# Diffusion backbone: Q, K and V ahead of the Fourier projection, attention units between its slabs, three conditioning units as TensorE products

## The chip, the cores and the metric

The kernel runs on one core of one Trainium2 chip. The metric is the device time of one execution in microseconds (us); lower is better. Five engines run side by side, each through its own instructions in order, and wait for each other by semaphores: TensorE (PE, matrix products into PSUM), VectorE (DVE), ScalarE (ACT), GpSimd (POOL), and SyncE (SP), which here only issues DMAs. All of the weights come from HBM once per execution.

## The reference, cut to what matters

Two layers over 256 tokens of width 2048, float32, and 256 context tokens. The change is in layer 0, the attention layer:

```
mod   = silu(c) @ w_mod[0] + b_mod[0]        # six vectors of 2048: shift, scale, gate (mixer), shift, scale, gate (MLP)
ux    = rmsnorm(x)*g0 * (1 + sc_m) + sh_m    # the same for the context, with silu(c_ctx)
f, q, k, v = split(ux @ att_w_in, [1024, 2048, 2304])      # 1024 Fourier columns, 1024 Q, 256 K, 256 V
k_c, v_c   = split(uc @ att_w_in[:, 2048:])
q, k  = rope(q), rope(k)
attn  = sink_softmax(window(q k^T), q k_c^T) @ [v, v_c]    # 8 heads, 2 KV heads, head 128
four  = real(fft over tokens and over the 256 channels of each of 4 groups of f)
x     = x + gt_m * rmsnorm(concat(four, attn) @ att_w_out)
x     = x + gt_f * rmsnorm(relu(modulate(x) @ w1)^2 @ w2)
```

Layer 1 has a short gated convolution instead of attention, and the same kind of MLP.

## The kernel before

**Weights.** Each product is computed to nearly float32 precision from a high and a low part. A weight *slab* is 256 rows by 512 columns, 512 KB: SP loads it into `raw` (4 slots), ScalarE writes its high part to `whi` (`hi`, line 716), VectorE the rest to `wlo` (`lo`, line 1014), TensorE takes three products: high by high, high by low, low by high. 8 slabs make a *group*, 512 output columns (`slab_of`, line 42, gives a group's first slab). `group_slab` (line 463) leaves channels on the partitions; `token_group` (line 520) leaves tokens there, with 12 products of 512 columns per slab. Slab w may be loaded when slab w - 4 is lowered, and split when slab w - 4 is used.

**Conditioning.** The vectors are products of one row with `w_mod`. A *unit* is half a vector: 16 slabs of 128 x 1024, 512 KB each. The first four units (mixer shift and scale) are TensorE products in the start phase (line 485), for both conditioning vectors, out of a ring in `early` (the memory of `h`): two products per slab with 32 stationary columns, each at its own column tile. The other 20 (`UNITS`) are VectorE's: `unit_slab` (line 1019) adds slab times scalar to `acc`; then GpSimd sums over partitions (line 1596) and, for a vector wanted by channel, multiplies by the identity; `finish_unit` (line 1072) reduces that and adds the bias. A gate is wanted by row and needs only the sum, `finish_gate` (line 1083). The slabs go through `mraw` (2 slots), or in attention through the 4 slots of `raw` (line 348).

**Layer 0's order.** Groups: two Fourier, two of Q, one of K and V with the context (`group_kv`, line 557), then attention with the DFTs, then four output groups. `UNIT_SHARE = (4, 6, 7, 7, 14)` puts 38 unit slabs beside the five input groups on VectorE (`att_group`, line 1220), the last 14 of them behind the last weight slab of the K and V group. VectorE copies K and rotates it behind these. `fin` holds the Fourier projection by channels. In attention, a *unit* `un` is one head and one half of the queries, 16 in all. TensorE's loop (line 648) has for each: transposes of the probabilities, `scores` of unit un + 3, one DFT part, and each second time the products with V. VectorE's loop (line 1285) has for each: denominator, maximum of unit un + 2, then three unit slabs of the 42 left. The transform over channels comes first, then that over tokens. V comes by channels, is copied and transposed (line 645). The output groups start when all of attention and the Fourier part is there (line 657).

The queues' order is what the program writes: SP issues loads in the order in which VectorE frees the slots, and waits in place; the units of the MLP and convolution stages run beside their weight slabs, with the same functions and places before and after the change.

Of the kernel before, what the change touches and what calls it, by code (L numbers as in the profile page):

```python
# [7 lines left out]
ALU = mybir.AluOpType  # L8
# [4 lines left out]
P = 128  # L13
# [22 lines left out]
PG_F, PG_Q, PG_KV, PG_WO = 0, 2, 4, 5  # L36
PG_MLP = (9, 57)
PG_CONV, PG_CO = 41, 53
W_F, W_KV = 0, 32


def slab_of(pg):

    return SL * pg + W_F
# [4 lines left out]
         (1, 3, 0), (1, 3, 1), (1, 4, 0), (1, 4, 1), (1, 5, 0), (1, 5, 1)]  # L49
GATES = (3, 4, 6, 11, 12, 13, 18, 19)  # L50
# [12 lines left out]
def by_tokens(pg):  # L63

    return PG_WO <= pg < PG_WO + 4 or PG_CO <= pg < PG_CO + 4 or any(
        pg0 <= pg < pg0 + 32 and (pg - pg0) % 8 >= 4 for pg0 in PG_MLP)
# [12 lines left out]
def masks_before(un):  # L79

    return un - sum(1 for g in GATES if g < un)

# [6 lines left out]
def backbone_program(nc, x_in, c_in, ctx_in, c_ctx, w_mod, b_mod, gains, att_w_in, sink, att_w_out,  # L89
                     conv_w_in, conv_w, conv_w_out, mlp_w1, mlp_w2, tables, out):  # L90
    with ExitStack() as ctx:
# [52 lines left out]
        fin = y[:, 8:16, :]  # L144
        qh = fq[:, 0:8, :]
        vsum = yf[:, 1024:2048].rearrange("p (g t) -> p g t", g=2)
        prob = [yf[:, 512 * i:512 * i + 512] for i in range(2)]
        probT = [ff[:, 2048 + 1024 * i:3072 + 1024 * i].rearrange("p (k q) -> p k q", k=4) for i in range(2)]
        ucs = yf[:, 1024:2048].rearrange("p (k n) -> p k n", k=2)
        row = (red[:, :], acc[:, 1, :])  # L150

        yt = yf.rearrange("p (a d) -> p a d", a=2)
        whole = [tmp[a][:, :, :].rearrange("p c t -> p (c t)") for a in range(2)]
# [19 lines left out]
        mid_landed = [sem(f"mid_landed{i}") for i in range(SLOTS)]  # L173
# [18 lines left out]
        v_t, v_ready = sem("v_t"), sem("v_ready")  # L192
# [52 lines left out]
        def _(sp):  # L245
# [21 lines left out]

            def w_slab(wt, row0, col0, s):
                return wt[bass.ds(row0 + s * CPS * P, CPS * P), bass.ds(col0, GW)].rearrange("(c p) n -> p c n", p=P)
# [20 lines left out]
            def stage_loads(w0, wt, row0, col0, un, n_m, l, mcol, ahead, early=False, gate_un=None):  # L290
# [3 lines left out]
                for i in range(4):  # L294
                    source = ahead if i == 3 else group_slabs(wt, row0, col0 + (i + 1) * GW)
                    k0, at = UNIT_EARLY[i] if early else (4 * i, UNIT_AT)
                    load_step(w0 + SL * (i + 1), source, un * UNIT + k0, k0, l, mcol, at if n_m else ())
# [4 lines left out]
            for w in range(START_SLABS):  # L302
                hv, k = divmod(w, KC)
                col0 = (1 - hv // 2) * D + (hv % 2) * HALF
                if w == START_F:
                    for s in range(SLOTS):
                        load_slab(W_F + s, s, group_slabs(att_w_in[0], 0, 0)(s))
# [10 lines left out]
            wi, wo = att_w_in[0], att_w_out[0]  # L318
# [17 lines left out]
            for s in range(SLOTS, SL):  # L336
                load_slab(W_F + s, s % SLOTS, group_slabs(wi, 0, 0)(s))

            m = 0
            for i in range(5):  # L340
                for s in range(SL):
                    if i < 4:
                        load_slab(W_F + SL * (i + 1) + s, s % SLOTS, group_slabs(wi, 0, (i + 1) * GW)(s))
                    for j in unit_places(i, s):
                        load_unit_slab(m + j, (m + j) % 2, 0, (m + j) % UNIT, mcol((m + j) // UNIT))
                m += UNIT_SHARE[i]

            for m in range(M_MID, M_WO):
                slot = (m - M_MID) % SLOTS
                if m < M_MID + SLOTS:  # L350
                    sp.wait_ge(lo_ready, W_KV + SLOTS + slot + 1)
                else:
                    sp.wait_ge(m_used, m - (SLOTS - 1))
                sp.dma_start(raw[:, slot, :], w_mod[0, m % UNIT * P:(m % UNIT + 1) * P,
                                                    mcol(m // UNIT):mcol(m // UNIT) + HALF]
                             ).then_inc(mid_landed[slot], 16)
            for s in range(SLOTS):
                sp.wait_ge(m_used, M_WO - (M_WO - 1 - M_MID - s) % SLOTS)
                load_slab(slab_of(PG_WO) + s, s, w_slab(wo, 0, 0, s))
            for s in range(SLOTS, SL):  # L360
                load_slab(slab_of(PG_WO) + s, s % SLOTS, w_slab(wo, 0, 0, s))
# [3 lines left out]
            stage_loads(slab_of(PG_WO), wo, 0, 0, U_WO, 4, 0, mcol(U_WO), group_slabs(mlp_w1[0], 0, 0), True,  # L365
# [25 lines left out]
            for t, (un, n_m, k0) in enumerate(CONV_PARTS):  # L391
                for j in range(3):
                    wt, col0 = ((ci, 2 * D + t * GW), (ci, t * GW), (ci, D + (t + 1) * GW) if t < 3 else (co, 0))[j]
                    w = slab_of(PG_CONV + 3 * t + j + 1)
                    for s in range(SL):
                        load_slab(w + s, s % SLOTS, w_slab(wt, 0, col0, s))
                        for i in conv_unit_slabs(SL * j + s, n_m):
                            load_unit_slab(UNIT * un + k0 + i, i % 2, 1, k0 + i, mcol(un))
# [13 lines left out]
        def _(pe):  # L412
# [65 lines left out]
            def first_group_slab(s):  # L478

                pe.wait_ge(lo_ready, W_F + s + 1)  # L480
                pe.wait_ge(u_ready, s + 1)
                group_slab(PG_F, 0, u, s)
# [37 lines left out]
            def token_group(pg, slot, src, slab_waits, closing=False):  # L520
# [4 lines left out]
                def products(s, a):  # L525
                    for c in range(CPS):
                        k = s * CPS + c
                        high = src[:, k, a * P:(a + 1) * P]
                        low = src[:, k, T + a * P:T + (a + 1) * P]
                        cols = slice(c * GW, (c + 1) * GW)  # L530
                        o = ps[:, 4 * slot + a, :]
                        pe.matmul(o, high, whi[:, s % SLOTS, cols], start=(k == 0), stop=False)  # L532
                        pe.matmul(o, high, wlo[:, s % SLOTS, cols], start=False, stop=False)  # L533
                        last = pe.matmul(o, low, whi[:, s % SLOTS, cols], start=False, stop=(k == KC - 1))  # L534
# [22 lines left out]
            def group_kv():  # L557


                for s in range(SL):  # L560
                    pe.wait_ge(lo_ready, W_KV + s + 1)
                    pe.wait_ge(c_ready, s // 2 + 1)
                    for c in range(CPS):
                        k = s * CPS + c
                        for m in range(4):
                            cols = slice(c * GW + m * P, c * GW + (m + 1) * P)
                            for i, src in enumerate((u, h)):
                                o = ps[:, 2 * i + m // 2, m % 2 * T:(m % 2 + 1) * T]
                                pe.matmul(o, whi[:, s % SLOTS, cols], src[:, k, 0:T], start=(k == 0 and m % 2 == 0),
# [1114 lines left out]
```

## Time and profile before

| | us |
|---|---|
| median of 3 runs (lowest, highest) | 2394.24 (2388.2, 2400.92) |
| the profiled execution | 2392.11 |
| its span (first to last instruction) | 2390.3 |
| TensorE busy | 2212.3 |
| weight loads (PEld) busy | 1832.3 |
| VectorE busy | 1736.6 |
| ScalarE busy | 994.9 |
| GpSimd busy | 180.9 |

Mean memory traffic is 248 GB/s, mean granted TensorE clock 0.964 of 2.4 GHz. Busy times of engines overlap, and TensorE's contain pipelined products whose ends are modelled. In a timeline row the number in brackets is idle time of the engine ahead of the piece, and what ended it; L427 and the like are lines of the kernel. Products of plain float32 operands appear as two instructions (x2) for each product. Stages of the span, from the timelines: start phase to 126.8 us; Fourier and Q groups to 209; K and V to 260.5; attention and DFTs 282.4 to 402.9; output groups 403.9 to about 506; the MLP of layer 0 from 526 us.

### The profile page before, as it was taken

The numbers are of one execution on the slowest core, as the hardware profiler recorded it, in microseconds if no ns is written. First come the engines' busy times: TensorE is split into PE (matmuls) and PEld (weight loads), VectorE is DVE, ScalarE is ACT, GpSimd is POOL, SyncE is SP. The second block draws the span as 40 slices with busy tenths as digits, with TensorE's granted clock in tenths as the row PEclk, the third lists the DMA queues.
The fourth block names the chain that finished last, engine by engine and source line by source line (L and its number), as shares of the span: only waits on it lengthen the run. The fifth ranks groups of instructions, "written<-read, shape, count | busy, mean of one in ns | idle before, by whom it ended". The sixth has DMA issues, their size and how long they took to land.

```text
span 2390.3 us, 30891 instructions
## 1 busy us (share of the span) xinstructions
PE 2212.3 (93%) x11279; PEld 1832.3 (77%) x11279; DVE 1736.6 (73%) x1830; ACT 994.9 (42%) x1214; POOL 180.9 (8%) x56
## 2 busy tenths in 40 slices
PE   6899577969999999999989999996999999999998
PEld 3488445758888888888878888875888888888886
DVE  0278595878879877978888998787887655555565
ACT  2155144434434434434444444433443443443443
POOL 0001020110102101101110110011010100000000
PEclk8999788989999999999999999998999999999999
DMA  9977576748888888888876787774888666656654
GB/s 377 347 251 251 177 234 205 266 150 278 287 288 276 278 293 275 276 296 300 277 274 222 274 298 272 244 262 153 284 278 303 186 191 191 187 190 193 204 192 142
DMA packets 253899, 592.67 MB, mean 248 GB/s; under 512 B 18082, under 2 KB 18610, under 8 KB 253234
## 3 DMA queue, kind: packets, MB, share of 16 engines
q1 hardware_dynamic: 253746, 590.63, 73.7%
q8 instruction: 96, 1.57, 0.3%
q14 instruction: 57, 0.47, 0.1%
HBM read 588.46 MB, written 2.10 MB: 247 GB/s over the span
## 4 chain that ended last, share of the span: by engine, by line
PE 75%; DVE 11%; DMA 6%; issue 5%; ACT 2%; POOL 1%; SPq 0%; DVEq 0%; ACTq 0%; POOLq 0%
PE ps L471 27%; PE ps L472 14%; PE ps L532 10%; PE ps L533 10%; PE ps L534 10%; DVE acc L1033 5%; DVE wlo L1017 2%; PE ps L427 2%; DMA early<-in_w_mod_dram 2%; DMA mraw<-in_w_mod_dram 2%; PE ps L498 1%; ACT whi L721 1%; POOL red L1596 1%; DMA raw<-in_conv_w_out_dram 1%; DMA raw<-in_att_w_out_dram 1%
## 5 line engine op out<-in xcount | busy, mean ns | idle before, releaser
L1017 DVE TENSOR_TENSOR wlo<-raw,whi 128x1024 fp32r<-128x1024 f32 x712 | 927.8, 1309 | 469.3 <-ACT whi L721 468.3
L721 ACT ACTIVATE whi<-raw 128x1024 fp32r<-128x1024 f32 x712 | 750.1, 1058 | 973.3 <-PE ps L534 380.1
L471 PE MATMUL ps<-u,whi 128*128 128x512 f32 x3072 | 1085.9, 398 | 13.6 <-DVE wlo L1017 11.3
L472 PE MATMUL ps<-u,wlo 128*128 128x256 f32 x3072 | 862.4, 281 | 0.0
L471 PEld LDWEIGHTS ps<-u,whi 128*128 128x128 f32 x3072 | 577.7, 188 | 159.0 <-DVE wlo L1017 12.5
L472 PEld LDWEIGHTS ps<-u,wlo 128*128 128x128 f32 x3072 | 581.4, 189 | 0.2
L532 PE MATMUL ps<-whi,h 128*128 128x512 f32 x1152 | 452.5, 393 | 16.4 <-DVE wlo L1017 16.4
L533 PE MATMUL ps<-wlo,h 128*128 128x512 f32 x1152 | 451.3, 392 | 0.0
L534 PE MATMUL ps<-whi,h 128*128 128x512 f32 x1152 | 450.9, 391 | 0.0
L1033 DVE SCALAR_TENSOR_TENSOR acc<-mraw,cs,acc 128x1024 f32<-128x1024 f32 x278 | 363.7, 1308 | 22.7 <-DMA mraw<-in_w_mod_dram 22.4
L532 PEld LDWEIGHTS ps<-whi,h 128*128 128x128 f32 x1152 | 218.1, 189 | 64.6 <-DVE wlo L1017 19.0
L534 PEld LDWEIGHTS ps<-whi,h 128*128 128x128 f32 x1152 | 218.1, 189 | 45.9
L533 PEld LDWEIGHTS ps<-wlo,h 128*128 128x128 f32 x1152 | 218.2, 189 | 45.0
L1596 POOL PARTITION_ALL_REDUCE red<-acc x20 | 129.1, 6457 | 1467.0 <-DVE acc L1033 612.7
L819 ACT ACTIVATE tmp<-ps 128x512 f32<-128x512 f32 x96 | 56.6, 596 | 42.3 <-PE ps L472 42.3
L427 PE MATMUL ps<-diag,x 128*128 128x128 f32 x256 | 39.9, 312 | 35.1 <-DVE diag L1126 35.1
L427 PEld LDWEIGHTS ps<-diag,x 128*128 128x128 f32 x256 | 36.5, 223 | 43.7 <-DVE diag L1126 36.3
L1033 DVE SCALAR_TENSOR_TENSOR acc<-raw,cs,acc 128x1024 f32<-128x1024 f32 x42 | 65.1, 1550 | 3.7
L532 PE MATMUL ps<-whi,u 128*128 128x512 f32 x128 | 52.4, 409 | 9.9 <-DVE wlo L1017 8.9
L498 PE MATMUL ps<-early,junk 128*32 128x512 f32 x192 | 42.2, 682 | 18.5 <-DMA early<-in_w_mod_dram 18.5
L957 ACT ACTIVATE h<-fq 128x512 fp32r<-128x512 f32 x64 | 39.5, 633 | 29.8 <-DVE fq L1445 29.8
L533 PE MATMUL ps<-wlo,u 128*128 128x512 f32 x128 | 51.6, 403 | 0.0
(149 smaller groups left out, 1195.5 us busy)
## 6 DMA issues: line engine op xcount, KB each, us to landing
raw<-in_mlp_w_dram SPq DMA_DIRECT2D x512, 512.0 KB, 4.6
mraw<-in_w_mod_dram SPq DMA_DIRECT2D x278, 512.0 KB, 5.0
raw<-in_conv_w_in_dram SPq DMA_DIRECT2D x96, 512.0 KB, 5.1
raw<-in_w_mod_dram SPq DMA_DIRECT2D x58, 512.0 KB, 4.7
early<-in_w_mod_dram SPq DMA_DIRECT2D x48, 512.0 KB, 9.8
raw<-in_att_w_in_dram SPq DMA_DIRECT2D x40, 512.0 KB, 5.4
raw<-in_att_w_out_dram SPq DMA_DIRECT2D x32, 512.0 KB, 5.9
raw<-in_conv_w_out_dram SPq DMA_DIRECT2D x32, 512.0 KB, 6.2
```

The source lines that it names most:

```text
L427: last = pe.matmul(ps[:, bank, c * T + a * P:c * T + (a + 1) * P], src[:, a, k * P:(k + 1) * P], diag[:, d0 + a, :], start=True, stop=True)
L471: pe.matmul(bank, whi[:, s % SLOTS, cols], src[:, k, :], start=(k == 0), stop=False)
L472: last = pe.matmul(bank[:, 0:T], wlo[:, s % SLOTS, cols], src[:, k, 0:T], start=False, stop=(k == KC - 1))
L498: last = pe.matmul(ps[tile:tile + 32, (0, 2, 0, 6)[hv] + n, :], crs[:, k, :], start_slab(w)[:, n * 512:(n + 1) * 512], start=(k < 4), stop ...
L532: pe.matmul(o, high, whi[:, s % SLOTS, cols], start=(k == 0), stop=False)
L533: pe.matmul(o, high, wlo[:, s % SLOTS, cols], start=False, stop=False)
L534: last = pe.matmul(o, low, whi[:, s % SLOTS, cols], start=False, stop=(k == KC - 1))
L721: act.activation(whi[:, s, :], raw[:, s, :], ACT.Copy).then_inc(hi_ready, 1)
L819: act.activation(tmp[half][:, :, :], right(slot, half), ACT.Copy).then_inc(b_copied, 1)
L1017: dve.tensor_tensor(wlo[:, s, :], raw[:, s, :], whi[:, s, :], ALU.subtract).then_inc(lo_ready, 1)
L1033: dve.scalar_tensor_tensor(out=a, in0=src, scalar=cs[:, bass.ds(k, 1)], in1=a, op0=ALU.mult, op1=ALU.add).then_inc(m_used, 1)
L1596: pool.partition_all_reduce(red[:, :], acc[:, un % 2, :], P, RADD).then_inc(unit_summed, 1)
```

## The change

Layer 0's order is changed; what lies behind its output groups is as before, but for slab counters.

- *Groups*: Q, Q, K and V, then Fourier, Fourier (`ATT_COLS` gives each group's first column). The Fourier groups are taken by tokens, so that the transform over tokens can come first (`token_dft`), then that over channels (`channel_dft`); V is taken by tokens too, and its transposes and copies through `vsum` go.
- *One loop of 24 steps*, t = 0..23, on TensorE, VectorE and ScalarE (25 there): a Fourier slab in steps 0 to 15 and one of the eight DFT parts of `DFT_ORDER` in steps 16 to 23; transposes of attention unit t - 4, scores of unit t - 2, in each second step the products with V; then conditioning slabs. In Fourier slabs banks 4 and 5 are used, scores alternate between banks 0 and 1, bank 2 has the transposes, 3 the attention output, 6 and 7 the conditioning products. The attention output goes to `h`, channels 8 to 15.
- *Conditioning*: units 3, 4 and 2 (`MIX_UNITS`) are TensorE products (`mix_slab`), two slabs per step, loaded into four slots of `early`, which is `h`'s memory and so only free when the K and V group is done. Units 0 and 1 are VectorE's, one slab per step up to step 15, two from 16 to 23; the first slab of each writes `acc`, the rest add to it. GpSimd takes no part in units 0 to 4. `unit_columns` turns units 0, 1 and 2 into columns by 24 products of two columns in slab 1 of the first output group; `spread_gate` spreads units 3 and 4 over the partitions by a product with a one-row matrix.
- *Output groups*: their slabs come attention half first (`OUT_ORDER`), waiting for each Fourier group in the second half. The loop has the lower halves of the first four of them.

The diff, cut to its core:

```diff
-PG_F, PG_Q, PG_KV, PG_WO = 0, 2, 4, 5
+PG_Q, PG_KV, PG_F, PG_WO = 0, 2, 3, 5
+ATT_COLS = (1024, 1536, 2048, 0, 512)
+MIX_UNITS = (3, 4, 2)
+DVE_FIRST = 2
+POOL_FIRST = 5
...
@@ SP
+            def mix_pair(n):
+                for i in (2 * n, 2 * n + 1):
+                    if i >= SLOTS:
+                        sp.wait_ge(mix_used, i - (SLOTS - 1))
+                    un, k = MIX_UNITS[i // UNIT], i % UNIT
+                    sp.dma_start(early[:, i % SLOTS, :], w_mod[0, k * P:(k + 1) * P, mcol(un):mcol(un) + HALF]
+                                 ).then_inc(mix_landed[i % SLOTS], 16)
...
+            for w in range(SLOTS, W_F + 6):
+                att_slab(w)
+            first_unit_slab(0)
+            first_unit_slab(1)
+            for t in range(-1, 17):
+                att_slab(W_F + t + 7)
+                if t == -1:
+                    sp.wait_ge(slab_used, W_KV + SL)
+                mix_pair(t + 1)
+                if t >= 0:
+                    first_unit_slab(t + 2)
+            for t in range(17, 23):
+                mix_pair(t + 1)
+                first_unit_slab(2 * t - 15)
+                first_unit_slab(2 * t - 14)
+            first_unit_slab(31)
             sp.wait_ge(o_ready, HEADS)
             sp.wait_ge(f_ready, FG)
             gate_rows(3)
...
@@ TensorE
+            def mix_slab(n):
+                i, k = divmod(n, UNIT)
+                if k == 0 and i:
+                    pe.wait_ge(mix_copied, i)
+                pe.wait_ge(mix_landed[n % SLOTS], 16 * (n // SLOTS + 1))
+                for half in range(2):
+                    tile = 32 * ((k + 2 * half) % 4)
+                    last = pe.matmul(ps[tile:tile + 32, 6 + half, :], crs[:, k, :],
+                                     early[:, n % SLOTS, half * 512:(half + 1) * 512], start=(k < 4),
+                                     stop=(k >= KC - 4), tile_position=(0, tile))
+                last.then_inc(mix_used, 1)
...
+            for t in range(24):
+                if t < 2 * SL:
+                    fourier_slab(t)
+                else:
+                    stage_dft, g = DFT_ORDER[t - 2 * SL]
+                    (channel_dft if stage_dft else token_dft)(g)
+                if 0 <= t - 4 < 2 * HEADS:
+                    turn_probs(t - 4)
+                if 0 <= t - 2 < 2 * HEADS:
+                    scores(t - 2)
+                if t >= 7 and t % 2 and t // 2 - 3 < HEADS:
+                    values(t // 2 - 3)
+                for n in mix_slabs(t):
+                    mix_slab(n)
...
+            def unit_columns():
+                pe.wait_ge(mix_copied, 3)
+                pe.wait_ge(m_used, DVE_FIRST * UNIT)
+                for un, src, pick in ((0, acc[:, 0, :], ones[:, 0:2]), (1, acc[:, 1, :], ones[:, 0:2]),
+                                      (2, mix_row[2], sel)):
+                    for c in range(KC // 2):
+                        last = pe.matmul(ps[:, 6, 16 * un + 2 * c:16 * un + 2 * c + 2], src[:, c * P:(c + 1) * P],
+                                         pick, start=True, stop=True)
+                last.then_inc(columns_done, 1)
+            def out_waits(s):
+                if s == 0:
+                    pe.wait_ge(o_ready, HEADS)
+                if s == 1:
+                    unit_columns()
+                    pe.wait_ge(pt_copied, 2 * HEADS)
+                    spread_gate(0, 2)
+                if s >= SL // 2:
+                    pe.wait_ge(f_ready, s - SL // 2 + 1)
+                if s == SL // 2 + 1:
+                    pe.wait_ge(mod_ready, 3)
+                    spread_gate(1, 6)
...
@@ ScalarE
+            for t in range(25):
+                if t in MIX_COPIES:
+                    copy_mix_row(MIX_COPIES.index(t))
+                if t <= 16:
+                    hi(W_F + 3 + t, (3 + t) % SLOTS)
+                if 0 <= t - 3 < 2 * HEADS:
+                    probabilities(t - 3)
+                if 0 <= t - 5 < 2 * HEADS:
+                    probs_turned(t - 5)
+                if t >= 8 and t % 2 == 0 and t // 2 - 4 < HEADS:
+                    o_high(t // 2 - 4)
+                if 0 <= t - 3 < 2 * HEADS:
+                    normalized(t - 3)
+                if 0 <= t - 2 * SL < 2 * FG:
+                    stage_dft, g = DFT_ORDER[t - 2 * SL]
+                    (fourier_high if stage_dft else token_transformed)(g)
...
@@ VectorE
+            for t in range(25):
+                if t in (SL, 2 * SL):
+                    take_fourier(t // SL - 1)
+                if 0 <= t - 3 < 2 * HEADS:
+                    row_max(t - 3)
+                if t <= 16:
+                    lo(W_F + 3 + t, (3 + t) % SLOTS)
+                if 0 <= t - 3 < 2 * HEADS:
+                    denominator(t - 3)
+                for m in first_unit_slabs(t):
+                    first_unit_slab(m)
+                if t >= 8 and t % 2 == 0 and t // 2 - 4 < HEADS:
+                    o_low(t // 2 - 4)
+                if 0 <= t - 2 * SL < 2 * FG and DFT_ORDER[t - 2 * SL][0]:
+                    fourier_low(DFT_ORDER[t - 2 * SL][1])
+            finish_first()
...
-UNIT_SHARE = (4, 6, 7, 7, 14)
-M_MID, M_WO = sum(UNIT_SHARE), UNIT * U_WO
+OUT_ORDER = tuple((s + SL // 2) % SL for s in range(SL))
+DFT_ORDER = ((0, 0), (0, 1), (1, 0), (0, 2), (1, 1), (0, 3), (1, 2), (1, 3))
+MIX_COPIES = (9, 17, 24)
+def mix_slabs(t):
+    return range(2 * (t - 1), 2 * t) if 1 <= t < 23 else range(44, 48) if t == 23 else ()
+def first_unit_slabs(t):
+    return (t,) if t < 16 else range(2 * t - 16, 2 * t - 14) if t < 24 else ()
```

The context pieces (`context_high`, `context_low`) come two per Q group now. Scores of unit un wait for the probabilities of unit un - 2, transposes for the copy of the ones before, `values` for the `o_low` of the head before.

## Rows read from the trace of the kernel before

**Rows 1.** The page: busy time (share) x instructions; the chain that ended last, by engine.

```profile
PE 2212.3 (93%) x11279; PEld 1832.3 (77%) x11279; DVE 1736.6 (73%) x1830; ACT 994.9 (42%) x1214; POOL 180.9 (8%) x56
...
PE 75%; DVE 11%; DMA 6%; issue 5%; ACT 2%; POOL 1%; SPq 0%; DVEq 0%; ACTq 0%; POOLq 0%
```

**Rows 2.** Busy time by stage: stretch, us, busy time (x instructions), clock, DMA share, GB/s.

```profile
47.00:92.00 45.00, 36.33 (x234) 16.11 (x232) 9.12 (x13) 7.57 (x8) 0.00 (x0) 0.98 0.98 372
...
164.80:187.00 22.20, 22.20 (x130) 19.58 (x129) 19.14 (x18) 13.25 (x17) 0.00 (x0) 1.00 0.90 330
...
212.60:260.50 47.90, 47.80 (x384) 47.62 (x384) 31.47 (x31) 10.35 (x13) 3.29 (x2) 0.96 0.66 207
260.50:282.40 21.90, 0.02 (x1) 0.02 (x1) 11.53 (x11) 5.27 (x9) 0.00 (x0) 0.60 0.72 240
282.40:404.00 121.60, 82.65 (x265) 50.99 (x266) 99.59 (x144) 49.99 (x116) 25.83 (x8) 0.83 0.62 199
```

**Rows 3.** The chain of waits in order of time: start us, us, what.

```profile
242.49 5.99 DMA mraw<-in_w_mod_dram
```

**Rows 4.** TensorE's timeline: start, us, line, shape, count, idle before and its releaser.

```profile
203.53 0.50 PE L471 MATMUL ps<-u,whi 128*128 128x512 f32 x1 [2.16 <-DVE wlo L1017]
...
212.68 0.36 PE L569 MATMUL ps<-u,whi 128*128 128x256 f32 x1 [3.23 <-DVE wlo L1017]
282.38 5.49 PE L598 MATMUL ps<-kv,fq 128*128 128x512 f32 x6 [21.91 <-DVE kv L1218]
```

**Rows 5.** Who waited for whom, 282 to 404 us: us in total, times, longest.

```profile
PE ps L606 <- ACT y L860: 36.9, 13, 6.5
ACT y L860 <- DVE sm L1271: 23.0, 11, 5.6
...
SPq L354 <- DVE acc L1033: 88.1, 38, 16.1
```

**Rows 6.** VectorE's timeline.

```profile
276.95 0.68 DVE L1250 COPY y<-ps 128x512 f32<-128x512 f32 x1
...
281.64 0.69 DVE L1218 TENSOR_TENSOR kv<-y 128x512 f32<-128x512 f32 x1
...
408.05 1.23 DVE L1017 TENSOR_TENSOR wlo<-raw,whi 128x1024 fp32r<-128x1024 f32 x1 [4.26 <-ACT whi L721]
410.77 1.23 DVE L1017 TENSOR_TENSOR wlo<-raw,whi 128x1024 fp32r<-128x1024 f32 x1 [1.50 <-ACT whi L721]
...
420.08 1.28 DVE L1033 SCALAR_TENSOR_TENSOR acc<-mraw,cs,acc 128x1024 f32<-128x1024 f32 x1
...
511.95 1.22 DVE L1077 TENSOR_REDUCE t<-red 128x8 f32<-128x1024 f32 x1 [10.05 <-POOL red L1601]
```

**Rows 7.** TensorE's operations one by one, from the same view of other stretches.

```profile
49.68 1.95 PE L438 MATMUL ps<-tab,red 128*128 128x2 f32 x16 [1.11 <-ACT red L761]
...
105.02 1.07 PE L498 MATMUL ps<-early,junk 128*32 128x512 f32 x8
106.01 0.50 PE L471 MATMUL ps<-u,whi 128*128 128x512 f32 x1
...
310.42 0.60 PE L606 MATMUL ps<-tab,y 128*128 128x128 f32 x4
...
310.85 1.02 PE L598 MATMUL ps<-kv,fq 128*128 128x512 f32 x2
...
311.71 1.89 PE L635 MATMUL ps<-tab,y 128*128 128x256 f32 x8
...
313.44 1.89 PE L615 MATMUL ps<-fq,kv 128*128 128x256 f32 x8
...
317.59 1.88 PE L624 MATMUL ps<-tab,y 128*128 128x512 f32 x4
```

**Rows 8.** The page's DMA issues: count, KB each, median us to landing.

```profile
mraw<-in_w_mod_dram SPq DMA_DIRECT2D x278, 512.0 KB, 5.0
...
early<-in_w_mod_dram SPq DMA_DIRECT2D x48, 512.0 KB, 9.8
```

More of the change, by code:

```diff
@@ L79, in masks_before, with first_slab @@
 def masks_before(un):
-    return un - sum(1 for g in GATES if g < un)
+    return un - POOL_FIRST - sum(1 for g in GATES if POOL_FIRST <= g < un)
+def first_slab(un):
+    return (un - len(MIX_UNITS)) * UNIT
 def unit_col(u):
@@ L348, in _ @@
[L348 to L356, printed above, removed]
@@ L640, in _ @@
-            for un in range(3):
-                scores(un)
-            pe.wait_ge(kv_copied, 3)
-            for kv in range(KV_HEADS):
-                for kt in range(4):
-                    last = pe.transpose(ps[:, kv, kt * P:(kt + 1) * P], vsum[:, kv, kt * P:(kt + 1) * P], ident)
-                last.then_inc(v_t, 1)
-            pe.wait_ge(v_ready, KV_HEADS)
-            for un in range(2 * HEADS):
-                turn_probs(un)
-                if un + 3 < 2 * HEADS:
-                    scores(un + 3)
-                (channel_dft if un % 4 < 2 else token_dft)(un // 4, un % 2)
-                if un % 2 == 1 and un >= 3:
-                    values(un // 2 - 1)
@@ L655, in _, with token_dft @@
-            values(HEADS - 1)
-            pe.wait_ge(f_ready, FG)
-            pe.wait_ge(o_ready, HEADS)
+            def token_dft(g):
+                pe.wait_ge(sum_done, sums_before(PG_F) + 2 * (g // 2 + 1))
+                if g == 0:
+                    pe.wait_ge(sum_done, sums_before(PG_F) + 4)
+                else:
+                    pe.wait_ge(fa_copied, 4 * g)
+                for m in range(2):
+                    for a in range(2):
+                        last = pe.matmul(ps[:, 4 + m, :], fin[:, a, g * T + m * P:g * T + (m + 1) * P], dft[:, a, :],
+                                         start=(a == 0), stop=(a == 1))
+                    last.then_inc(fa_done, 1)
@@ new lines, in spread_gate @@
+            def spread_gate(i, bank):
+                pe.wait_ge(first_row_ready, 1)
+                for n in range(2):
+                    last = pe.matmul(ps[:, bank + n, :], first_row, mix_row[i][:, n * 512:(n + 1) * 512],
+                                     start=True, stop=True)
+                last.then_inc(gate_spread, 1)
+            def unit_columns():
[7 more added lines that the diff above has]
+                last.then_inc(columns_done, 1)
@@ L1245, in _ @@
             dve.wait_ge(tab_landed, 32)
-            for i in range(5):
-                att_group(i)
+            for i in range(2):
+                query_group(i)
+            for s in range(3):
+                lo(W_F + s, s)
             dve.wait_ge(slab_used, W_KV + SL)
@@ L1618 @@
 CONV_PARTS = ((14, 16, 0), (15, 16, 0), (16, 8, 0), (16, 8, 8))
-def unit_places(i, s):
-    n = UNIT_SHARE[i]
-    return range(s * n // SL, (s + 1) * n // SL)
 def conv_unit_slabs(i, n_m):
```

393 lines of the change are left out of this document (202 added, 191 removed).

## The prediction, made before the changed kernel was built or run

> **What bounds the kernel now.** I read the page first: TensorE is busy for 93% of the span and owns 75% of the chain that ended last [rows 1]. Such a kernel gains only where TensorE is not working, so I asked next for busy time by stage [rows 2]. In the projection groups up to 209 us TensorE is busy but for short waits. The key and value group (212.6 to 260.5 us) is full too, by weight loads: 47.62 of 47.9 us. Then come the two loose stretches. From 260.5 to 282.4 us TensorE does nothing (0.02 us); from 282.4 to 404.0 us, in attention with the DFTs, it is busy 82.65 of 121.6 us, at a granted clock of 0.83. Together these are 143.5 us (260.5 to 404.0). The chain of waits says why in the first one: VectorE waits for one conditioning slab after the other, such as the one of 5.99 us [rows 3]. TensorE itself starts again 21.91 us late, for the rotated keys that VectorE makes only behind these slabs [rows 4]. In the second one TensorE waits for normalized probabilities (36.9 us over 13 waits), ScalarE for VectorE's reciprocals, and the DMA queue for VectorE to free slabs, 88.1 us over 38 waits [rows 5]. VectorE, with 99.59 of 121.6 us busy, sets the order. The memory is not full there: DMA share 0.62, 199 GB/s [rows 2].
>
> **The change part by part.** The working is against the profiled execution: span 2390.3 us, its own time 2392.1 us; the median of the runs, 2394.2 us, is 0.1% above that.
>
> *Front: Q, K, V ahead of the Fourier groups.* Two Fourier groups of 22.2 us (two windows alike, 142.6:164.8 and 164.8:187.0, one shown [rows 2]) leave the stretch before K and V: -44.4 us, to be paid back below. No conditioning slab lies in this stretch any more, so VectorE, which ran such slabs ahead of the weight halves that TensorE waited for 2.16 and 3.23 us [rows 4], has none of them: -5.4 us. What is late next there is TensorE's own work; the second context piece per group costs ScalarE and VectorE a few us beside groups in which they are busy 13.25 and 19.14 of 22.2 us, slabs included [rows 2]. If that cover failed, the loss would be the same 5 us again. K and V keep their 384 products of 256 columns; V by tokens only swaps the operands: 47.9 us, no change. So K and V end 49.8 us earlier, at about 211 us.
>
> *The joint stretch: 24 steps of TensorE.* It holds, at full clock:
> - 16 Fourier slabs of 12 products of 512 columns. The output projection has the same slab, and its lower halves follow TensorE at 2.72 us, from 408.05 to 410.77 [rows 6]: 43.5 us.
> - 16 transposes of probabilities at 0.43 us, 16 scores at 0.86, 8 value products at 1.73, and 16 DFT parts (8 of each kind, same counts as before) at 1.73 [rows 7], start to start, the value product taken as long as the DFT part since both show 1.89 us busy: 6.9 + 13.8 + 13.8 + 27.7 = 62.2 us.
> - 48 conditioning slabs as products, in 24 pairs. A pair in the start phase takes from 105.02 to 106.01 us, 0.99 us [rows 7], though it is eight products of 512 columns: their 32-column tiles run side by side. 23.8 us. These are new on TensorE.
> The sum is 129.5 us. The eight V transposes go.
>
> The granted clock: it was 0.83 where TensorE was 68% busy, 0.96 to 1.00 where it was full [rows 2]. Here it should be about 85% busy; I take 0.93, so 129.5 / 0.93 = 139 us. The Trainium skill has a rule that speaks against the change here (TensorE: Matmul & The Clock Gate, "HAM oscillation"): short bursts of products with DMA waits between them fall back to 1.2 GHz again and again. By that rule the whole would end near rival 3's 2407 us.
>
> To this I add waits, 11 us: about 3 us at the start, since the second pair of conditioning slabs is queued on SP behind a weight slab that needs ScalarE and VectorE to finish keys and rotation first (in the kernel before this took from 276.95 to 282.33 us, VectorE's copy to its last add [rows 6]); 2 us for the two Fourier evictions that must precede the next group in the same banks; 6 us in steps 17 to 23, where SP asks for VectorE's second slab of a step only after TensorE has finished that step's products, it lands about 5.0 us later [rows 8], and the steps' o_low stands behind it on VectorE, for which `values` waits. That gives 150 us.
>
> *The DMA side of it.* From the end of K and V on SP moves 17 weight slabs, 48 slabs into `early` and 30 into `mraw` beside one weight slab loaded ahead: 96 x 0.524 MB = 50.3 MB. At the 372 GB/s of 47:92 [rows 2] this is 135 us, at the 330 GB/s of the 164.8:187.0 window 152 us. So DMA and TensorE are about equal, and 150 us fits both.
>
> *VectorE* there has 32 slabs at 1.28 us and 17 lower halves at 1.23 [rows 6], 62 us. Before, its 99.59 us held 42 slabs and 4 lower halves, 59 us, so attention's own part is some 41 us. Sum about 103 of 150 us, so it is hidden. If it were late by a step, attention's chain would be next (rival 1).
>
> So the loose 143.5 us and the 44.4 us of Fourier become 150 us.
>
> *Output projection.* Its first half of rows is the attention half, so it needn't wait for the last DFTs; this is why I charge no wait at its start. New on TensorE, in its first group: 24 column products. Eight of the same kind took 16 instructions and 1.95 us from 49.68 us on [rows 7]: 5.9 us. Two spread products of two 512-column halves each, at the 0.86 us of a score: 3.4 us. And TensorE waits for VectorE's slab 31, which is asked for only when slab 29 is used: about 2.5 us (none, if TensorE is slower before). Sum +12 us; bounds are 9 without the wait and 18 with the column products at half the clock. SP's `gate_rows(3)` waits behind these columns, and the weight slabs of group 1 behind it on the queue; TensorE then still has 7 slabs of 2.72 us, 19 us, so it isn't late. In return POOL does units 3 and 4 no longer. That was off the path: only the last unit's reduction ends it, VectorE waiting 10.05 us for it until 511.95 [rows 6]. Unit 5, its slabs and this wait stay as they are, so the boundary behind it stays too, and all that follows.
>
> Sum: -49.8 + (150 - 143.5) + 12 = -31 us, so 2361 us.
>
> **The rivals.**
> 1. *The attention chain keeps its pace.* Score, maximum, exponential, reciprocal, scaling, transpose cross five engines; one transpose bank now serves where two did. Before, a unit took 121.6 / 16 = 7.6 us [rows 2]. 24 steps at this pace are 182 us: 2361 + 32 = 2393 us, no change. For it: VectorE still has rows, lower halves and slabs in line. Against: a step now has one slab of VectorE (1.3 us), not three (3.8 us), and the DMA queue's 88 us of waiting for VectorE [rows 5] falls to a third.
> 2. *Everything packs.* DMA at 372 GB/s is the only bound and the waits fall inside: 136 us, and no wait for slab 31: 2361 - 14 - 3 = 2344 us. For it: ten slab buffers keep the queue full. Against: one queue in order, and each of its waits holds all behind it.
> 3. *Slower: TensorE waits for slabs it now consumes itself and runs at the half clock.* Place: `mix_slab`, two per step, in the queue ahead of every other product. In the start phase, where it also ate slabs, the landing took 9.8 us [rows 8]. If it waits in each step, its busy share falls under that of the attention before. At a clock of 0.70, 129.5 / 0.70 + 11 = 196 us: 2407 us. It decides from a clock of 0.71 on (193 us, +12 us); up to 0.76 it only eats the gain. Against it: a pair is asked for two steps ahead, about 10 us, and in 47:92, with TensorE fed in this way, the clock was 0.98.
>
> **How the numbers follow.** Forecast 0.60 (its own range 2348 to 2380 us), rival 1 0.19, rival 2 0.12, rival 3 0.09. About 0.5%, 12 us, is what a measurement of this kernel can tell from no change: under 2380 us is faster, over 2404 slower. Forecast and rival 2 with a little of rival 1 give faster 0.74; the rest of rival 1, same 0.17; rival 3, slower 0.09. The range goes from rival 2 with the low bound of the output term, 2341 us, to rival 1, 2394 us.
>
> **What would show it.** K and V end near 211 us; no idle of 20 us behind it; the first product of the output projection near 361 us; DMA share near 0.9 and a clock over 0.9 in between; that projection some 12 us longer, with 48 small products in it. Were the stretch over 180 us, TensorE's waits would name the cause: for ScalarE's probabilities (rival 1) or for `early` (rival 3). A first stretch that ends after 216 us, or a changed time behind the first boundary, would make the working wrong in a place where I saw nothing.

## The result and the profile after

The changed kernel takes 2380.7 us (median of 10 runs, 2373.63 to 2383.16), the kernel before 2393.7 us (also of 10) beside it: ratio 0.9946, 95% interval 0.9929 to 0.9962, so 13 us faster. The forecast was 31 us. The direction is right and the outer range, 2341 to 2394 us, holds the time, but 2380.7 us lies just outside the forecast's own range of 2348 to 2380 us, and the gain is less than half of the one forecast.

The page of the changed kernel, span 2379.9 us: busy times, and the chain that ended last [rows 1]:

```profile
PE 2239.5 (94%) x11455; PEld 1833.0 (77%) x11455; DVE 1656.3 (70%) x1780; ACT 993.0 (42%) x1211; POOL 140.8 (6%) x43
...
PE 79%; DVE 7%; DMA 7%; issue 3%; ACT 2%; POOL 1%; SPq 1%; DVEq 0%; ACTq 0%; POOLq 0%
```

TensorE has 27 us more of work (new products) in a shorter span. Busy time by stage of the changed kernel, columns as in [rows 2]:

```profile
128.00:211.50 83.50, 82.04 (x577) 77.04 (x578) 43.79 (x50) 47.00 (x64) 0.00 (x0) 0.98 0.52 158
211.50:307.10 95.60, 90.32 (x430) 54.84 (x428) 64.20 (x114) 51.64 (x96) 0.00 (x0) 0.98 0.92 345
307.10:382.30 75.20, 54.49 (x216) 28.62 (x212) 23.63 (x34) 18.38 (x43) 0.00 (x0) 0.89 0.61 219
382.30:511.80 129.50, 106.37 (x440) 85.80 (x440) 85.78 (x104) 44.62 (x68) 11.18 (x5) 0.88 0.60 207
```

From 211.5 to 307.1 us, steps 0 to 15, TensorE is busy 90.32 of 95.6 us, and DMA share and traffic, 0.62 and 199 GB/s in the old attention [rows 2], are 0.92 and 345 GB/s. But from 307.1 to 382.3 us, steps 16 to 23, TensorE is busy 54.49 of 75.2 us, at a clock of 0.89, and the DMA share is back at 0.61. Marks of both kernels, from TensorE's timelines, beside the forecast:

| us from the span's start | before | forecast | after | after less forecast |
|---|---|---|---|---|
| K and V end | 260.5 | 211 | 211.5 | +0.5 |
| step 16 begins | - | 307 | 307.1 | 0 |
| first product of the output projection | 403.9 | 361 | 382.4 | +21 |
| first product of the MLP's boundary | 521.0 | 490 | 511.8 | +22 |
| end of the span | 2390.3 | 2359 | 2379.9 | +21 |

(The 307 of the forecast follows from its own prices: 84.3 of the 129.5 us lie in steps 0 to 15, at 0.93 and with 5 of the 11 us of waits that is 95.6 us.) One stretch, steps 16 to 23, holds nearly the whole error of 21 us. Its chain of waits in the changed kernel (start us, us, what), from TensorE's conditioning pair of step 18 on:

```profile
333.94 1.94 PE ps L652 x8
335.88 0.28 SPq L365
336.20 0.43 SPq L365
336.68 5.61 DMA mraw<-in_w_mod_dram
342.31 1.28 DVE acc L1152
343.59 0.35 DVE h L1396
344.07 3.39 PE ps L683 x8
347.46 1.07 PE ps L652 x8
348.53 0.28 SPq L365
348.86 0.43 SPq L365
349.33 5.65 DMA mraw<-in_w_mod_dram
355.00 1.30 DVE acc L1152
356.32 4.19 DMA mraw<-in_w_mod_dram
360.53 1.29 DVE acc L1152
361.82 0.35 DVE h L1396
362.30 3.75 PE ps L683 x8
366.05 1.77 PE ps L652 x8
```

It is a ring. L652, the conditioning pair at the end of TensorE's step, frees its slots; SP (L365) then issues the next pair, and only behind it VectorE's slabs; one lands 5.6 us later; VectorE adds it (L1152), then makes `o_low` of that step (L1396), for which the value products (L683) of TensorE's next odd step wait; at their end stand the conditioning pair and SP again. Around 335.88 to 348.53 us it takes 12.65 us, and 19.3 us from 348.53 to 367.82, two steps, where two slabs land one after the other (5.65 and 4.19 us). TensorE's work in a step is about 5.6 us.

Until 333 us the ring takes another way back to TensorE. The row maximum of the next attention unit also stands behind the slabs in VectorE's order; ScalarE's exponential waits for it, the copy of the turned probabilities (L980) stands behind that exponential, and TensorE's next transposes (L674) wait for the copy. The turn before the one above:

```profile
323.36 5.37 DMA mraw<-in_w_mod_dram
...
328.75 1.28 DVE acc L1152
...
330.04 0.22 DVE ps L1380
...
330.28 0.70 DVE sm L1382
...
331.01 0.23 DVE sm L1384
...
331.46 0.76 ACT y L967 x2
332.22 0.50 ACT fq L980
...
332.85 1.09 PE ps L674 x4
```

The waits of 307 to 383 us name both places (us, times, longest): 9.3 us for `o_low` and 8.3 us for the copy. The DMA rates in 40 slices of 305 to 382 us show bursts at 400 GB/s between zeros:

```profile
DVE acc L1152 <- DMA mraw<-in_w_mod_dram: 49.0, 8, 10.2
...
PE ps L683 <- DVE h L1396: 9.3, 2, 5.6
PE ps L674 <- ACT fq L980: 8.3, 2, 6.7
```

```profile
GB/s 400 175 326 402 349 334 404 36 0 66 355 417 251 0 4 9 64 387 419 219 0 0 0 219 404 423 383 385 264 100 0 0 0 202 415 413 347 358 328 126
```

### The profile page after: what moved, and what is told of

It is laid out like the page before. It is cut to its first block, busy times and chain, and to the rows that moved or that the text cites. A ratio compares the mean times of both kernels' runs of the same rounds, so it can differ in the third digit from the quotient of the medians.

```text
span 2379.9 us, 31101 instructions
## 1 busy us (share of the span) xinstructions
PE 2239.5 (94%) x11455; PEld 1833.0 (77%) x11455; DVE 1656.3 (70%) x1780; ACT 993.0 (42%) x1211; POOL 140.8 (6%) x43
## 4 chain that ended last, share of the span: by engine, by line
PE 79%; DVE 7%; DMA 7%; issue 3%; ACT 2%; POOL 1%; SPq 1%; DVEq 0%; ACTq 0%; POOLq 0%
PE ps L497 26%; PE ps L498 13%; PE ps L560 10%; PE ps L562 10%; PE ps L561 10%; DMA mraw<-in_w_mod_dram 3%; DVE wlo L1129 2%; PE ps L453 2%; DVE acc L1139 2%; DMA early<-in_w_mod_dram 2%; PE ps L524 1%; ACT whi L827 1%; DMA raw<-in_conv_w_in_dram 1%; DMA raw<-in_mlp_w_dram 1%; PE ps L683 1%
## 5 line engine op out<-in xcount | busy, mean ns | idle before, releaser
L497 PE MATMUL ps<-u,whi 128*128 128x512 f32 x2944 | 1040.2, 398 | 12.9 <-DVE wlo L1129 10.2
L498 PE MATMUL ps<-u,wlo 128*128 128x256 f32 x2944 | 825.3, 280 | 0.0
L497 PEld LDWEIGHTS ps<-u,whi 128*128 128x128 f32 x2944 | 554.3, 188 | 152.7 <-issue 12.1
L498 PEld LDWEIGHTS ps<-u,wlo 128*128 128x128 f32 x2944 | 557.3, 189 | 0.2
L560 PE MATMUL ps<-whi,h 128*128 128x512 f32 x1216 | 477.2, 392 | 18.2 <-DVE wlo L1129 16.2
L561 PE MATMUL ps<-wlo,h 128*128 128x512 f32 x1216 | 475.3, 391 | 0.0
L562 PE MATMUL ps<-whi,h 128*128 128x512 f32 x1216 | 475.3, 391 | 0.0
L560 PEld LDWEIGHTS ps<-whi,h 128*128 128x128 f32 x1216 | 229.7, 189 | 70.0 <-DVE wlo L1129 18.8
L562 PEld LDWEIGHTS ps<-whi,h 128*128 128x128 f32 x1216 | 229.5, 189 | 48.2
L1732 POOL PARTITION_ALL_REDUCE red<-acc x15 | 96.7, 6446 | 1248.2 <-DVE acc L1139 558.4
L1152 DVE SCALAR_TENSOR_TENSOR acc<-mraw,cs,acc 128x1024 f32<-128x1024 f32 x30 | 38.5, 1284 | 65.3 <-DMA mraw<-in_w_mod_dram 65.0
L1574 DVE TENSOR_TENSOR fq<-ps,tmp 128x512 f32<-128x512 f32 x64 | 43.1, 686 | 10.4 <-ACT tmp L925 10.4
L1031 ACT ACTIVATE fq<-tmp 128x512 f32<-128x512 f32 x32 | 20.0, 624 | 61.3 <-DVE tmp L1452 38.3
```

The source lines that it names most:

```text
L497: pe.matmul(bank, whi[:, s % SLOTS, cols], src[:, k, :], start=(k == 0), stop=False)
L498: last = pe.matmul(bank[:, 0:T], wlo[:, s % SLOTS, cols], src[:, k, 0:T], start=False, stop=(k == KC - 1))
L560: pe.matmul(o, high, whi[:, s % SLOTS, cols], start=first, stop=False)
L1732: pool.partition_all_reduce(red[:, :], acc[:, un % 2, :], P, RADD).then_inc(unit_summed, 1)
```

## The experiments

Theory: SP's one queue, in order, ties VectorE's slabs to TensorE's step end, and VectorE's order ties `o_low` and the row maxima to the slabs. Rivals: the memory can't deliver the bytes of these steps, or the DFT parts, handed between TensorE and ScalarE, set 9 us a step. Medians below stand beside 2393.6 to 2395.1 us of the kernel before in the same sessions.

**SP's order in steps 17 to 22.**

```diff
             for t in range(17, 23):
-                mix_pair(t + 1)
                 first_unit_slab(2 * t - 15)
                 first_unit_slab(2 * t - 14)
+                mix_pair(t + 1)
```

> SP's order alone, steps 17 to 22: the two VectorE slabs are asked for before the TensorE pair. Queue theory (the pair's wait for the end of TensorE's step holds the VectorE slabs behind it, these hold o_low, and o_low holds the value products): steps 16 to 23, 75 us in the changed kernel, fall to 52 to 60 us, and the kernel to 2358 to 2366 us. Bandwidth theory (the slabs' bytes fill the memory): order changes nothing, 2381 us. DFT theory (TensorE and ScalarE hand the transforms to and fro at some 9 us a step): nothing, 2381 us.

2360.72 us, ratio 0.9867 (0.9849 to 0.9884). The output projection begins at 365.1 instead of 382.4 us, and steps 16 to 23 last 57.3 instead of 75.3 us. The same bytes in the same queue, another order: 17 us on the trace, 20 in the median. Its row from 307.1 to 360 us, columns as in [rows 2]:

```profile
307.10:360.00 52.90, 47.41 (x204) 26.44 (x196) 23.81 (x35) 16.44 (x41) 0.00 (x0) 0.97 0.88 306
```

The memory moves 306 GB/s there, so it could deliver all along; and the DFT parts were not touched. Both rivals fall as the cause of these 17 us. The ring isn't wholly gone: TensorE still waits 1.59 and 2.15 us for `o_low`.

**VectorE's order from step 16 on**: `o_low` and `fourier_low` ahead of the step's slabs.

```diff
-                for m in first_unit_slabs(t):
-                    first_unit_slab(m)
+                if t < 2 * SL:
+                    for m in first_unit_slabs(t):
+                        first_unit_slab(m)
...
                     fourier_low(DFT_ORDER[t - 2 * SL][1])
+                if t >= 2 * SL:
+                    for m in first_unit_slabs(t):
+                        first_unit_slab(m)
```

> VectorE's order alone, from step 16 on: o_low and fourier_low before the step's slabs. Queue theory: the waits of TensorE's value products for o_low (3.7 and 5.6 us) and for the output projection go, but VectorE still falls behind on its slabs, so the last row maxima stay late: 8 to 12 us less, 2369 to 2373 us. Bandwidth and DFT theory: 2381 us.

2371.74 us, 0.9910 (0.9893 to 0.9926): 9 us off, as the queue theory had it. The waits for `o_low` are gone; the one in front of the last transposes, the ring's other way, stays:

```profile
331.91 1.08 PE L674 MATMUL ps<-tab,y 128*128 128x128 f32 x4 [6.79 <-ACT fq L980]
```

Steps 16 to 23 last 61.6 us here, 13.7 less than in the changed kernel, but some of it is lost again behind them: the column products wait 3.75 us for slab 31, where it was 1.70 us.

**Both orders.**

> Both orders together. Queue theory: the last steps run at TensorE's own work of some 49 us plus DMA, little better than the SP order alone: 2355 to 2364 us. Bandwidth and DFT theory: 2381 us.

2361.07 us, 0.9858 (0.9842 to 0.9875), equal to SP's order alone, and steps 16 to 23 last 57.2 us. SP's order acts on both ways of the ring, VectorE's only on the one through `o_low`. With both the last waits for `o_low` are gone too, but the last pair for TensorE now comes later in SP's queue, and its wait takes their place:

```profile
360.93 3.21 PE L652 MATMUL ps<-early,junk 128*32 128x512 f32 x8 [3.87 <-DMA early<-in_w_mod_dram]
```

**Without the loads.** SP's loads of slabs 17 to 31 go, and VectorE doesn't wait:

```diff
-                dve.wait_ge(m_landed[m % 2], 16 * (m // 2 + 1))
+                if m < 17:
+                    dve.wait_ge(m_landed[m % 2], 16 * (m // 2 + 1))
+                else:
+                    src = acc[:, 0, :]
```

> The loads of VectorE's slabs 17 to 31 are left out, and VectorE takes its own accumulator in their place (conditioning units 1 and the mixer's output thus wrong). Queue theory: no slab to wait for, the last eight steps take some 50 us: about 2355 us. Bandwidth theory: the same, 15 of 31 slabs gone, so this run and the order runs together separate the two. DFT theory: the steps stay near 9 us, 2375 us or more.

2355.11 us, 0.9832 (0.9809 to 0.9854). Its row of the same stretch:

```profile
307.10:360.00 52.90, 51.92 (x238) 29.67 (x238) 27.29 (x37) 19.62 (x44) 0.00 (x0) 1.00 0.53 174
```

From step 16 to the output projection it takes 48.8 us (306.9 to 355.8). TensorE's own work there is 45.2 us by the forecast's prices at full clock, and the granted clock is 1.00 here, so 3.6 us remain for waits (0.79 and 0.19 us for `early` are seen) and for hand-overs between products. The forecast's 48.6 us, at a clock of 0.93, come out the same by luck. The prices of the products were about right, and what was missing was a wait.

**Another queue.** VectorE's 32 slabs are issued by GpSimd, which has nothing to do there; SP keeps all other loads and waits.

```diff
+            for m in range(DVE_FIRST * UNIT):
+                if m >= 2:
+                    pool.wait_ge(m_used, m - 1)
...
+                pool.dma_start(mraw[:, m % 2, :], w_mod[0, k * P:(k + 1) * P, c0:c0 + HALF]
+                               ).then_inc(pm_landed[m % 2], 16)
```

> The changed kernel with VectorE's 32 slabs issued from GpSimd's queue, which is idle in this stretch, instead of SP's; the order of all waits of SP's other loads stays. Queue theory: these slabs are no longer behind the TensorE pairs, so the tail shrinks as with SP's order changed: 2358 to 2368 us. Bandwidth theory: the same bytes at the same places, 2381 us. If GpSimd's way of issuing costs VectorE or itself much, 2381 us or more, with a full DMA share in the last steps and no zeros in it.

2356.39 us, 0.9840 (0.9818 to 0.9861). Nothing of the order of work on an engine changed, only who asks:

```profile
307.10:360.00 52.90, 51.05 (x230) 27.67 (x229) 26.14 (x37) 17.05 (x43) 7.42 (x14) 1.00 0.93 324
```

TensorE is busy 51.05 of 52.9 us, at 0.93 DMA share and 324 GB/s. Steps 16 to 23 last 49.9 us (309.9 to 359.8) with every slab loaded, 1.1 us more than without VectorE's loads. So neither the bytes nor the two slots of `mraw` set the pace of these steps; SP's queue did. The time lies below the 2358 to 2368 us expected: SP's order leaves 57.3 us there, this queue 49.9. The intervals of this one and of SP's order overlap; I don't call the whole kernel faster than that.

**Column products.** The +12 us of the output projection were forecast as a sum, and came as one: 129.4 us from its first product to the boundary's, 117.1 before. But the parts are not those of the sum. TensorE's timeline of the changed kernel:

```profile
387.06 6.18 PE L746 MATMUL ps<-tab,acc 128*128 128x2 f32 x32 [1.70 <-DVE acc L1152]
393.11 3.55 PE L746 MATMUL ps<-tab,y 128*128 128x2 f32 x16
396.52 3.76 PE L735 MATMUL ps<-red,diag 128*128 128x512 f32 x4
```

24 column products take 9.6 us (5.9 forecast) and the first spread product some 3 us to the next slab's (1.7). The granted clock is 1.00 from 382.4 to 387.0 us and 0.57, 0.50 and 0.50 in these three rows. In the kernel with both orders:

```profile
367.06 3.63 PE L746 MATMUL ps<-tab,acc 128*128 128x2 f32 x32
370.55 2.96 PE L746 MATMUL ps<-tab,y 128*128 128x2 f32 x16
373.38 3.76 PE L735 MATMUL ps<-red,diag 128*128 128x512 f32 x4
```

The first 32 instructions (16 column products) go at 0.11 us each, at a granted clock of 1.00; then the next 16 take 2.96 us at 0.61, and the spread product, two products of 0.86 us at the full clock [rows 7], takes some 2.8 us to the next slab's at 0.50, the level of 1.2 GHz. So I took the columns eight at a time, behind slabs 0, 1 and 2, and the spread behind slab 3:

```diff
-                if s == 1:
-                    unit_columns()
+                if s in (1, 2, 3):
+                    unit_columns((0, 2, 1)[s - 1])
+                if s == 4:
                     pe.wait_ge(pt_copied, 2 * HEADS)
                     spread_gate(0, 2)
```

> Both orders together, and besides the 24 column products are taken eight at a time behind output slabs 0, 1 and 2, the spread product behind slab 3. Theory one (the small products let the granted clock fall to 1.2 GHz and that makes them and the spread product dear: 9.6 us instead of 7.6 at full clock, and some slab products after it at the lower clock): 3 to 5 us less than both orders alone, 2356 to 2358 us. Theory two (their number costs, 0.12 us each at any rate): no change, 2361 us.

2355.29 us, 0.9834 (0.9815 to 0.9852). The granted clock is 1.00 from 367.7 to 384.0 us, and all four go at the full rate:

```profile
367.71 1.84 PE L746 MATMUL ps<-tab,acc 128*128 128x2 f32 x16
...
372.28 1.84 PE L746 MATMUL ps<-tab,y 128*128 128x2 f32 x16
...
376.85 1.84 PE L746 MATMUL ps<-tab,acc 128*128 128x2 f32 x16
...
381.42 1.88 PE L735 MATMUL ps<-red,diag 128*128 128x512 f32 x4
```

The trace has the boundary 3.0 us earlier (487.4 for 490.4 us), the medians say 5.8, with intervals that overlap those of both orders alone. The expected effect is seen in the rows, and theory two falls; its size is 3 us or a little more, 3 to 5 having been expected.

**Nearly no column and spread products**, on top of both orders.

```diff
-                    for c in range(KC // 2):
+                    for c in range(1):
...
-                for n in range(2):
+                for n in range(1):
                     last = pe.matmul(ps[:, bank + n, :], first_row, mix_row[i][:, n * 512:(n + 1) * 512],
```

> Both orders together; of the column products one in eight is left, of the spread products one of two halves (most of units 0, 1 and 2 and half of each gate thus missing). If the prediction's +12 us for the output projection is right, of which 9 are these products: 2361 - 8 = 2353 us. If GpSimd's reduction of unit 5 ends the projection anyway, the boundary stays where it is: 2358 to 2361 us.

2354.72 us, 0.9826 (0.9802 to 0.9851): 6 us in the medians, and in the traces the projection lasts 116.2 instead of 126.3 us, 10 us. GpSimd's reduction of unit 5 doesn't hide them; that part of the forecast's term stands.

**What bounds steps 0 to 15.** First half of the products of a conditioning slab:

```diff
-                for half in range(2):
+                for half in range(1):
                     tile = 32 * ((k + 2 * half) % 4)
```

> Both orders together; of each conditioning slab on TensorE only the first half is multiplied (half of units 3, 4 and 2 missing), all slabs are still loaded. If TensorE bounds the joint stretch: a pair in 24 steps falls from 0.99 to some 0.5 us, -10 us, 2351 us. If the memory does (share 0.92 in steps 0 to 15): 0 to -3 us, 2358 to 2361 us, with the idle time on TensorE. If column tiles run side by side, four products of half the tiles could take as long as eight: then no change either, but with TensorE as busy as before.

2360.56 us, 0.9860 (0.9838 to 0.9882), no change, and for the third reason named, so it tells nothing of the bound: the pair is as long with two products (four instructions) as with four (eight instructions). In both, each column tile in use takes one product of the pair.

```profile
250.82 1.05 PE L652 MATMUL ps<-early,junk 128*32 128x512 f32 x4
```

Then with 128 of 512 columns in all of them:

```diff
-                    last = pe.matmul(ps[tile:tile + 32, 6 + half, :], crs[:, k, :],
-                                     early[:, n % SLOTS, half * 512:(half + 1) * 512], start=(k < 4),
+                    last = pe.matmul(ps[tile:tile + 32, 6 + half, 0:128], crs[:, k, :],
+                                     early[:, n % SLOTS, half * 512:half * 512 + 128], start=(k < 4),
```

> Both orders together; each product of a conditioning slab on TensorE takes 128 instead of 512 columns (three quarters of units 3, 4 and 2 missing), in the same tiles, all slabs still loaded. A pair falls from 0.99 to about 0.3 us, 16 us in all. If TensorE bounds the joint stretch, steps 0 to 15 get 10 us shorter and the kernel is at 2345 to 2350 us. If the memory does: 2356 to 2361 us, the DMA share stays at 0.92 or rises, and the idle time appears on TensorE.

2359.47 us, 0.9852 (0.9836 to 0.9868), inside what was expected of the memory as bound. The pair is short now:

```profile
255.35 0.43 PE L652 MATMUL ps<-early,junk 128*32 128x128 f32 x8
```

The stretch from 235 to 300 us, columns as in [rows 2], of this kernel and then of the one with both orders:

```profile
235.00:300.00 65.00, 59.87 (x325) 40.61 (x324) 45.76 (x86) 38.51 (x76) 0.00 (x0) 1.00 1.01 380
```

```profile
235.00:300.00 65.00, 63.09 (x312) 38.43 (x311) 44.88 (x84) 35.91 (x70) 0.00 (x0) 1.00 0.98 369
```

Step 16 comes 4.1 us earlier in these two traces (302.7 for 306.8), of 9.5 us that TensorE has less to do by then (15 pairs, 1.06 less 0.43 us each); the share goes to 1.01 and the idle time to TensorE. So both bounds lie close to each other in steps 0 to 15, and they take turns. With both orders, the memory moves 401 GB/s at a share of 1.02 from 222 to 254 us, while TensorE is busy 27.61 of 32 us; from 254 to 307 us TensorE is busy 52.41 of 53 us, with 358 GB/s. That moving more of VectorE's slabs into these steps would not pay is my reading of this; no run shows it.

**The kernel before, with one number changed.**

```diff
-UNIT_SHARE = (4, 6, 7, 7, 14)
+UNIT_SHARE = (6, 8, 8, 7, 9)
```

> The kernel BEFORE with one number changed: 6, 8, 8, 7, 9 conditioning slabs beside the five input groups instead of 4, 6, 7, 7, 14. If the 22 idle us after K and V are the 14 slabs alone (2.6 us each), five fewer there give -8 to -13 us less 1 to 4 us in fuller groups: 2382 to 2390 us. If the memory cannot give more in the groups (share 0.90 there): they get longer by as much, 2392 to 2396 us.

2388.9 us beside 2395.1, 0.9975 (0.9963 to 0.9987). The idle time ahead of attention falls from 21.91 us [rows 4] to 10.79, the 11 us of five slabs. But the groups in front lose much of it, in three waits of 3.02, 3.39 and 2.26 us for VectorE's lower halves, with VectorE busy 69.13 of 82.2 us (columns as in [rows 2]):

```profile
126.80:209.00 82.20, 72.56 (x389) 62.35 (x390) 69.13 (x64) 47.29 (x60) 9.34 (x3) 0.94 0.79 275
209.00:262.00 53.00, 50.74 (x371) 48.59 (x371) 40.80 (x41) 18.39 (x24) 0.00 (x0) 0.94 0.68 222
```

K and V end at 270.9 instead of 260.5 us, 3.2 us of which are a later first group in this execution, which is the second slowest of the eleven (2394.85 us). So spreading alone is worth a quarter of a per cent, 6 us in the medians.

**The mends together**: GpSimd's queue, `o_low` first, columns eight at a time.

> The changed kernel with the three mends at once: VectorE's slabs from GpSimd's queue, o_low ahead of the slabs, column products eight at a time. Queue theory: the two do not overlap in what they save: 2356 less 4 to 6 us, 2350 to 2352 us. If the queue mend already took what the columns lose (TensorE warmer there): 2355 us.

2352.65 us (2348.85 to 2353.49), 0.9818 (0.9803 to 0.9832): the fastest of all, 42 us under the kernel before and 28 under the changed one. It is 3.7 us under the queue alone, a little less than the 4 to 6 us expected, and the two intervals overlap, so that the mends add up is likely but not shown. In its trace TensorE still waits 3.15 and 1.14 us for the last pair in `early`. Whether more slots for `mraw` would loosen the ring under SP's queue was not run.

## Why the prediction was wrong

*Front*: right. K and V end at 211.5 us, forecast 211. Both waits of [rows 4] are gone but for one of 1.21 us, and the second context piece per group cost nothing to be seen.

*Joint stretch, steps 0 to 15*: right to the microsecond, in part by luck. The waits are 5.3 us (2.76 for the second pair in `early`, 0.93 for a Fourier eviction, 0.98 and 0.60 in front of transposes), priced at 5. The clock is 0.98 instead of 0.93, and about as much, some 4 us, is lost in hand-overs between products, which the prices left out. Two errors that cancel.

*Joint stretch, steps 16 to 23*: this step failed. It is the term "6 us in steps 17 to 23, where SP asks for VectorE's second slab of a step only after TensorE has finished that step's products". The wait was named, with SP, the landing, `o_low` and `values`, but given 6 us without a working. It is a closed ring, and so it isn't a delay but the period of the loop: landing, addition, `o_low`, value products, conditioning pair, issue, 12.7 us for a step and 19.3 us for two, instead of 5.6 and 11 us of work. The ring's other way, by row maximum, exponential and copy to the transposes, was not in the term at all; with `o_low` out of it, the stretch still lasts 61.6 us. The ring cost 26.5 us over the same steps without those loads (75.3 against 48.8), where 6 were priced. SP's order alone brings the kernel to 2360.7 us, beside the 2361 of the forecast. That is near, but not proof of every term: in its trace the stretch lasts 57.3 us (54.6 forecast) and the output projection 126.1 us (129.1 forecast).

*The clock of 0.93*: it was 0.89 in these steps and 1.00 in the same steps from GpSimd's queue, so the loss came with the ring's idle time: value products of 3.39 and 3.75 us instead of 1.73. That part is inside the 26.5. The rule that the prediction cites against the change, short bursts with waits between them, did not show in steps 0 to 15 (0.98); in steps 16 to 23 the products behind TensorE's waits of 3.73 and 5.56 us did run at half rate.

*Output projection*: +12.3 us against +12, by other parts: columns and the first spread some 5 us dearer, the wait for slab 31 1.70 us instead of 2.5. Of what came back, 2.6 us are seen in the waits: 8.0 us for lower halves instead of 8.9, and 13.40 us at the boundary instead of 15.10. Why they are shorter, and the rest, is open. From the boundary's first product to the end: 1868.1 us against 1869.3, no change, as forecast.

*Rivals*: rival 1 (attention's chain at its old pace) was not it in steps 2 to 15, which had scores in them and were full. Its sign did show in steps 17 and 18, 8.3 us in front of the transposes, but as a way of the ring: the argument against it, "a step now has one slab of VectorE", holds only up to step 15, from 16 on there are two. Rival 2's even packing was not reached: share 0.61 in steps 16 to 23, and 0.93 once GpSimd issues the slabs. Rival 3's place was near, SP's queue with TensorE's slabs in it, but the wait was for VectorE's slabs, and in the changed kernel never for `early` beyond 2.76 us.

*A count*: the "eight products" of a conditioning pair are four, in eight instructions, as plain float32 operands take two each. The 0.99 us were read from the trace, so the sum doesn't change.

## What to carry to other kernels

When one DMA queue serves two consumers, list for each load what the queue waits for before it, and follow whether that leads back to the load's own consumer: if so, add up the ring once around and compare it with the step's work. Where the sum is larger, as here (12.7 against 5.6 us), it sets the period. Look for every way back, not only the first one found: here there were two. The ring was loosened by the order of one queue and cut by a second queue, with the same bytes and work.

## What the runs showed of the hardware

- In a row of products with two moving columns TensorE's clock fell though the profile shows no idle time: with both orders, 32 instructions in 3.63 us at a granted clock of 1.00, then 16 in 2.96 us at 0.61, and a spread product at 0.50, which is 1.2 GHz; with slab products between them, three times 16 in 1.84 us each, at 1.00. The Trainium skill has the fall after an idle stretch (TensorE: Matmul & The Clock Gate, "What's actually happening"); here it comes while TensorE is counted as busy.
- Products in 32-column tiles of 512 moving columns: four of two slabs, in all four tiles, take 1.06 us, and two, in two of the tiles, 1.05 us. Leaving tiles empty gains nothing; 128 moving columns in all four take 0.43 us.
- The load rate was 401 to 405 GB/s over 32 us (222 to 254 us, DMA share 1.02 to 1.03, in the changed kernel and in that with both orders). The 364 to 380 GB/s of 235 to 300 us are a mean with pauses in it.
- GpSimd issued a slab in 0.53 us of its time, and neither VectorE's adds (1.28 us each) nor the landings of its slabs (6.4 us in the median from 211 to 360 us, with either queue) became slower.
